# Paged decode attention: another place for the pages, another order of values and scores, a maximum per row

## The chip, the cores and the metric

One core of a Trainium2 chip runs the whole step as one program. The metric is the device time of one execution in microseconds; less is better.

## The reference

One step of a hybrid layer: a prompt of 1024 tokens and eight decode tokens go through a combined projection, latent attention beside a state-space mixer, an output projection, a mixture of experts and a last gate. The change touches only the attention of the eight decode tokens. Each of them (a "sequence") has 4096 cached tokens in 32 pages of 128, found by a page table; a cached token is a latent of 256 values and a rotary key of 32.

```python
past_ckv = cache_ckv[page_table].reshape(B, -1, KV_LORA)      # B = 8, 4096 x 256
past_kr = cache_krope[page_table].reshape(B, -1, QK_ROPE)     # 4096 x 32
q_lat = jnp.einsum('blhd,chd->blhc', q_nope, w_uk)            # 8 heads
s_past = (jnp.einsum('blhc,btc->bhlt', q_lat, past_ckv)
          + jnp.einsum('blhr,btr->bhlt', q_rope, past_kr)).astype(jnp.float32) * ATTN_SCALE
s_new = ...                                                   # the token itself
p = jax.nn.softmax(jnp.concatenate([s_past, s_new], axis=-1), axis=-1)
o_lat = (jnp.einsum('bhlt,btc->blhc', p[..., :T], past_ckv)
         + jnp.einsum('bhls,bsc->blhc', p[..., T:], ckv))
return jnp.einsum('blhc,chd->blhd', o_lat, w_uv)
```

The sum over cached tokens does not depend on their order, so a page may lie in memory in any way that scores and values share.

## The kernel before

The program is a row of stages (projection, prompt attention, decode attention, output projection, experts, last gate), each a block with an instruction stream per engine, written out by hand with semaphores; a barrier of all engines ends each. The decode stage (lines 1434 to 1681) begins at about 572 us and its last VectorE instruction ends at 783.55 us.

**Pages.** Eight pages make a group, four groups a sequence, 32 groups in all. A page is 128 tokens of 288 floats (147,456 bytes) and is one DMA (`load_pages`, line 1252): token p of the page goes to partition p, 1,152 bytes in each of 128 partitions. SP issues pages 0 to 3 of a group and POOL 4 to 7 (`SHARE`, line 1250); page numbers are read from the table into registers first. Groups 0 to 3 are loaded by SP alone during the prompt attention. The ring has 11 places (`RING3`). Group `at` from 11 on waits in `load_share` (line 1266) until the sequence that used its place is done with its values: `spv_mm` counts the sequences whose last matmul (line 1531) is finished. So the end of sequence b releases four groups: the last one of sequence b + 2 and the first three of sequence b + 3.

**Transposes.** VectorE turns each group (`turn_pages`, line 1617: one 32x32 block transpose of 128x2304) into `pgT`, which has room for one sequence; a group's half of `pgT` must have been scored before (`past_mm`).

**Scores.** `scores(b)` on TensorE (line 1483) works in 32x32 tiles in two halves of two groups each, 144 instructions a half, and then the new token (line 1496). They stand in four PSUM banks; partition 32 g + h holds head h for group g, so a head's scores are spread over four partitions.

**Softmax.** `largest(b)` on VectorE (line 1623) takes a maximum per partition (`smx`), with the new token's for heads. To make it one per head, TensorE transposes `smx` (`largest_row`, 1500), VectorE takes the maximum over the four parts (`row_bounds`, 1636), TensorE brings it back as a column (`bound_column`, 1504), and ACT copies it to `nb`. Only then does ACT take the exponentials (`exps`, 1580), with sums per partition in `rs`. TensorE turns the probabilities (`turn_probs`, 1508) and adds the sums of a head's four partitions, ACT copies the turned ones (`turned_probs`, 1592), VectorE takes the reciprocal and the new token's turned probabilities (`row_sums`, 1646).

**Values.** `weigh(b)` (line 1520) multiplies the turned probabilities with the pages as loaded, 32 matmuls of two instructions, and the new token (1531). ACT scales the result by the reciprocal (`latent_out`, 1598).

**Order.** On TensorE, for each b: scores of b, turning of b - 1, `largest_row` of b, first half of the values of b - 1, `bound_column` of b, second half of the values of b - 1. On VectorE: transposes 0 and 1 of sequence b + 1, maximum of b, sums of b - 1, `row_bounds` of b, transposes 2 and 3. On ACT: copy of the turned probabilities of b - 1, exponentials of b, scaled result of b - 1. Queues run in order, so an instruction that waits holds all behind it.

Of the kernel before, what the change touches and what calls it, by code (L numbers as in the profile page):

```python
# [78 lines left out]
def program(nc, t_in, t_out):  # L79
# [16 lines left out]
    with ExitStack() as ctx:  # L96
# [1155 lines left out]
        def load_pages(eng, name, at, first, some):  # L1252
# [3 lines left out]
            for m, page in enumerate(found):  # L1256
                eng.dma_start(group_pages(at)[:, first + m, :], cache[bass.ds(page, 1), :, :].rearrange("a p w -> (a p) w")).then_inc(page_sw[at % RING3] if name == "pool" else page_in[at % RING3], 16)  # L1257
# [188 lines left out]
        smx = sb_in(p3, "smx", [P, 1])  # L1446
# [6 lines left out]
        rs = sb_in(p3, "rs", [P, 2])  # L1453
# [19 lines left out]
        def _(pe):  # L1473
# [34 lines left out]
            def turn_probs(b):  # L1508
                pe.wait_ge(S("sexp_rdy"), 2 * b + 2)
                if b:  # L1510
                    pe.wait_ge(S("pT_rdy"), b)
                    pe.wait_ge(S("rden3_rdy"), b)
                for x in range(8):
                    last = pe.matmul(pb[:, 4, 32 * x:32 * x + 32], pexp[:, x, :, :].rearrange("p g t -> p (g t)"), heads, start=True, stop=True)
                last.then_inc(S("pT_tr"), 1)
                for m in range(2):
                    pe.matmul(pb[:, 5, H:H + 1], same[:, :, :].rearrange("p c r -> p (c r)"), rs[:, m:m + 1], start=m == 0, stop=m == 1, skip_group_check=True)
                pe.transpose(pb[0:32, 5, 0:H], pnew[:, :], ident[0:H, 0:H]).then_inc(S("sums_mm"), 1)

            def weigh(b, some):  # L1520
# [4 lines left out]
                for x in some:  # L1525
                    q = x % 4
                    last = pe.matmul(pb[32 * q:32 * q + H, 7, 0:KL], pT[b % 2][:, x % 8, x // 8, :], group_pages(4 * b + x // 8)[:, x % 8, 0:KL], start=x < 4,
                                     stop=x >= PAGES - 4 and q > 0, skip_group_check=True, tile_position=(0, 32 * q))
                if some[-1] == PAGES - 1:
                    pe.wait_ge(S("pTn_rdy"), b + 1)  # L1530
                    pe.matmul(pb[0:H, 7, 0:KL], pTn[:, :], ckvn[:, :], start=False, stop=True, skip_group_check=True,
                              tile_position=(0, 0)).then_inc(S("spv_mm"), 1)
# [1353 lines left out]
```

## Time and profile before

| | |
|---|---|
| median of three runs | 1594.5 us (1593.17 to 1598.28) |
| the profiled execution | 1593.95 us, its span 1592.3 us |
| decode stage in the trace | about 572 to 784 us |
| transposes of pages (line 1621) | 32, 81.8 us busy on VectorE, idle before them 83.4 us |
| matmuls of the scores (line 1492) | 2304, 79.1 us busy, idle before them 44.6 us |
| matmuls of the values (line 1527) | 512, 34.4 us busy |
| turning of the probabilities (line 1514) | 128, 15.8 us busy |
| exponentials (line 1588) | 8, 8.9 us busy |

Engines are PE (TensorE), PEld (its weight loads), DVE (VectorE), ACT, POOL and SP; a "q" behind a name is the engine's sequencer. In a timeline a line merges neighbouring instructions of one kind, with their number behind the x; "idle before" is what the engine waited and for whom. PEclk is the granted TensorE clock (1.0 is 2.4 GHz, 0.5 is 1.2 GHz).

### The profile page before, as it was taken

To read this page: it belongs to the slowest core of one execution; us is meant where nothing else is said; L and a number is where in the kernel's file an instruction comes from. 1 tells how busy PE (TensorE), PEld (TensorE's weight loads), DVE (VectorE), ACT (ScalarE), POOL (GpSimd) and SP (SyncE) were. 2 spreads that over 40 slices of the span, in tenths; PEclk is the share of its full clock that TensorE was granted. 3 is DMA by queue.
4 is the path that set the end of the run, shared out by engine and by line. 5 is a ranking of instruction groups with operands and counts; after the bars stand their busy time and mean duration, and the time that the engine had idled before them with its cause. 6 is when DMAs were issued, how large, how long until landed. Compare 5 with 4: busy or idle time off the path is not lost. (4 is left out here: it accounts for less than half of the span.)

```text
span 1592.3 us, 26749 instructions
## 1 busy us (share of the span) xinstructions
PE 1354.5 (85%) x9613; PEld 1084.7 (68%) x9613; DVE 979.7 (62%) x1338; ACT 638.1 (40%) x856; POOL 220.3 (14%) x322
## 2 busy tenths in 40 slices
PE   5989999786688877766789982899999999937997
PEld 4989999776344444333568872687888888825886
DVE  5456556663577765454244445788888888845653
ACT  5222434320366611101232100777777777743221
POOL 6000221051100032232000000000000000012210
PEclk9999999898799988878779995899999999977999
DMA  5121111375994055464262221479656999935410
GB/s 185 31 79 41 57 67 54 126 251 155 283 371 113 1 169 161 143 217 152 80 226 106 96 90 66 148 263 363 230 211 235 331 404 405 379 143 214 159 67 40
DMA packets 121049, 275.20 MB, mean 173 GB/s; under 512 B 23601, under 2 KB 44594, under 8 KB 120626
## 3 DMA queue, kind: packets, MB, share of 16 engines
q1 hardware_dynamic: 100578, 200.64, 37.1%
q0 software_dynamic: 17200, 61.63, 10.9%
q10 hardware_dynamic: 3168, 11.54, 1.8%
q8 instruction: 67, 1.10, 0.3%
q14 instruction: 36, 0.29, 0.1%
HBM read 214.34 MB, written 58.38 MB: 171 GB/s over the span
## 5 line engine op out<-in xcount | busy, mean ns | idle before, releaser
L399 PE MATMUL pb<-xH,wH 128*128 128x344 f32 x432 | 143.1, 331 | 25.1 <-DVE wL L858 11.0
L401 PE MATMUL pb<-xH,wL 128*128 128x344 f32 x432 | 140.8, 326 | 0.0
L400 PE MATMUL pb<-xL,wH 128*128 128x344 f32 x432 | 140.8, 326 | 0.0
L1621 DVE STREAM_TRANSPOSE pgT<-pages 128x2304 f32<-128x2304 f32 x32 | 81.8, 2570 | 83.4 <-DMA pages<-in_cache 74.5
L2463 DVE TENSOR_TENSOR downL<-raw_down,downH 128x2048 fp32r<-128x2048 f32 x44 | 98.9, 2288 | 45.2 <-ACT downH L2365 45.2
L1492 PE MATMUL pb<-pgT,q 32*8 32x256 f32 x2304 | 79.1, 432 | 44.6 <-DVE pgT L1621 41.9
L2365 ACT CAST gateH<-raw_gate 128x2048 fp32r<-128x2048 f32 x44 | 83.9, 1911 | 67.5 <-PE pb L2298 41.5
L2463 DVE TENSOR_TENSOR gateL<-raw_gate,gateH 128x2048 fp32r<-128x2048 f32 x44 | 100.5, 2287 | 15.8 <-ACT gateH L2365 15.8
L399 PEld LDWEIGHTS pb<-xH,wH 128*128 128x128 f32 x432 | 83.8, 194 | 27.3 <-issue 10.9
L2463 DVE TENSOR_TENSOR upL<-raw_up,upH 128x2048 fp32r<-128x2048 f32 x44 | 100.3, 2281 | 1.0 <-ACT upH L2365 1.0
L1492 PEld LDWEIGHTS pb<-pgT,q 32*8 32x8 f32 x2304 | 41.5, 94 | 81.8 <-DVE pgT L1621 44.9
L1321 PE MATMUL pb<-kh,qh 96*128 96x512 f32 (+3 forms) x192 | 75.8, 515 | 15.5 <-DMA vh<-v_d 14.5
L2365 ACT CAST upH<-raw_up 128x2048 fp32r<-128x2048 f32 x44 | 81.6, 1902 | 15.8 <-PE pb L2298 15.8
L400 PEld LDWEIGHTS pb<-xL,wH 128*128 128x128 f32 x432 | 83.7, 194 | 0.0
L401 PEld LDWEIGHTS pb<-xH,wL 128*128 128x128 f32 x432 | 83.6, 194 | 0.0
L2365 ACT CAST downH<-raw_down 128x2048 fp32r<-128x2048 f32 x44 | 81.6, 1909 | 0.0
L1257 POOL DMA_DIRECT2D pages<-in_cache x112 | 60.2, 538 | 117.2 <-issue 113.1
L2296 PE MATMUL pb<-gateH,hxH 128*128 128x512 f32 x176 | 73.5, 417 | 1.3 <-ACT sg L2378 0.7
L2296 PE MATMUL pb<-downH,axH 128*128 128x512 f32 x176 | 72.2, 410 | 1.6 <-DVE axL L2477 1.6
L2297 PE MATMUL pb<-gateL,hxH 128*128 128x512 f32 x176 | 71.3, 405 | 0.0
L2298 PE MATMUL pb<-gateH,hxL 128*128 128x512 f32 x176 | 71.0, 403 | 0.0
L1368 ACT ACTIVATE prob<-pb,nmx 128x128 f32<-128x128 f32 (+7 forms) x64 | 47.7, 745 | 57.8 <-DVE nmx L1402 56.6
(436 smaller groups left out, 3246.7 us busy)
## 6 DMA issues: line engine op xcount, KB each, us to landing
raw_gate<-in_w_gate SPq DMA_DIRECT2D x32, 1024.0 KB, 7.4
raw_up<-in_w_up SPq DMA_DIRECT2D x32, 1024.0 KB, 7.8
raw_down<-in_w_down SPq DMA_DIRECT2D x32, 1024.0 KB, 8.0
pages<-in_cache SPq DMA_DIRECT2D x144, 144.0 KB, 3.6
y_d<-yzero POOLq DMA_DIRECT2D x4, 4096.0 KB, 31.7
pages<-in_cache POOLq DMA_DIRECT2D x112, 144.0 KB, 3.7
y_d<-yo ACTq DMA_DIRECT2D x22, 512.0 KB, 4.1
wraw_p<-in_w_blk SPq DMA_DIRECT2D x18, 512.0 KB, 3.5
```

The source lines that it names most:

```text
L399: pe.matmul(out, wh, xh, start=first, stop=False)
L400: pe.matmul(out, wh, xl, start=False, stop=False)
L401: return pe.matmul(out, wl, xh, start=False, stop=last)
L1257: eng.dma_start(group_pages(at)[:, first + m, :], cache[bass.ds(page, 1), :, :].rearrange("a p w -> (a p) w")).then_inc(page_sw[at % RING3 ...
L1321: last = pe.matmul(pb[:, bank, 0:w], qh[b][n][:, i * P:(i + 1) * P], kh[b][n][:, 512 * m:512 * m + w], start=True, stop=True)
L1492: last = pe.matmul(pb[32 * g:32 * g + H, r, 0:256], q4[at, b, j, :], pgT[at, 8 * g:8 * g + 8, 32 * j:32 * j + 32], start=j == 0, stop=j == ...
L1621: dve.transpose(pgT[:, 8 * g:8 * g + 8, :], group_pages(4 * b + g)).then_inc(S("pgT_rdy"), 1)
L2296: pe.matmul(out, xh[:, k, :], high[w][:, k, a:b], start=first, stop=False)
L2297: pe.matmul(out, xh[:, k, :], low_[w][:, k, a:b], start=False, stop=False)
L2298: return pe.matmul(out, xl[:, k, :], high[w][:, k, a:b], start=False, stop=last)
L2365: act.copy(part(high[w], c), part(raw[w], c)).then_inc(S(w + "_high"), 1)
L2463: dve.tensor_tensor(part(low_[w], c), part(raw[w], c), part(high[w], c).bitcast(F32), ALU.subtract).then_inc(S(w + "_low"), 1)
```

## The change

A page goes into 32 partitions: page n of a group to the set 32 (n mod 4), with four tokens (4,608 contiguous bytes) in each partition. It is still one DMA per page, by the same queues.

Each partition keeps its own maximum: the exponentials take its negative (`nmx3`) and start without the head's maximum. That one is found in the same steps as before, but enters later as a factor per partition, exp of the partition's maximum less the head's (`part_w`, on ACT): the row sums are multiplied by it (`part_s`, on VectorE) before TensorE adds them, and the reciprocal is multiplied by it (`scale_rdy`).

The order on TensorE for each b becomes: second half of the values of b - 1, turning of b, `largest_row` of b, first half of the values of b, `bound_column` of b, scores of b + 1, sums of b. `spv_mm` counts halves. A half of the values is now four page columns of all four groups, so all places of a sequence are released by its second half. On VectorE one transpose instead of two stands ahead of the maximum, and the transpose of the new token's probabilities is copied by ACT instead of VectorE.

```diff
             for m, page in enumerate(found):
-                eng.dma_start(group_pages(at)[:, first + m, :], cache[bass.ds(page, 1), :, :].rearrange("a p w -> (a p) w")).then_inc(...)
+                n = first + m
+                dst = group_pages(at)[32 * (n % 4):32 * (n % 4) + 32, n // 4 * 4:n // 4 * 4 + 4, :]
+                eng.dma_start(dst, cache[bass.ds(page, 1), :, :].rearrange("a (p s) w -> (a p) s w", s=4)).then_inc(...)
...
             if at >= RING3:
-                eng.wait_ge(S("spv_mm"), (at - RING3) // 4 + 1)
+                eng.wait_ge(S("spv_mm"), 2 * ((at - RING3) // 4) + 2)
...
-                pe.transpose(pb[0:1, 6, 0:P], smx[:, :], ident).then_inc(S("smx_tr"), 1)
+                pe.transpose(pb[0:1, 6, 0:P], smx[:, b % 2:b % 2 + 1], ident).then_inc(S("smx_tr"), 1)
...
                 for x in range(8):
-                    last = pe.matmul(pb[:, 4, 32 * x:32 * x + 32], pexp[:, x, :, :]..., heads, start=True, stop=True)
-                last.then_inc(S("pT_tr"), 1)
+                    pe.matmul(pb[:, 4, 32 * x:32 * x + 32], pexp[:, x, :, :]..., heads, start=True, stop=True)
+                pe.transpose(pb[0:32, 4, 256:256 + H], pnew[:, :], ident[0:H, 0:H]).then_inc(S("pT_tr"), 1)
+
+            def sums(b):
+                pe.wait_ge(S("part_s_rdy"), b + 1)
                 for m in range(2):
-                    pe.matmul(pb[:, 5, H:H + 1], same..., rs[:, m:m + 1], start=m == 0, stop=m == 1, ...)
-                pe.transpose(pb[0:32, 5, 0:H], pnew[:, :], ident[0:H, 0:H]).then_inc(S("sums_mm"), 1)
+                    last = pe.matmul(pb[:, 5, H:H + 1], same..., part_s[:, m:m + 1], start=m == 0, stop=m == 1, ...)
+                last.then_inc(S("sums_mm"), 1)
...
                 for x in some:
-                    q = x % 4
-                    last = pe.matmul(pb[32 * q:32 * q + H, 7, 0:KL], pT[b % 2][:, x % 8, x // 8, :], group_pages(4 * b + x // 8)[:, x % 8, 0:KL], ...)
-                if some[-1] == PAGES - 1:
+                    for c in range(4):
+                        last = pe.matmul(pb[32 * c:32 * c + H, 7, 0:KL], pT[b % 2][:, x, c, :], group_pages(4 * b + c)[:, x, 0:KL], ...)
+                if some[-1] == 7:
                     pe.wait_ge(S("pTn_rdy"), b + 1)
...
-            largest_row(0)
-            bound_column(0)
-            for b in range(1, NB + 1):
-                if b < NB:
-                    scores(b)
-                turn_probs(b - 1)
-                if b < NB:
-                    largest_row(b)
-                weigh(b - 1, range(0, PAGES // 2))
-                if b < NB:
-                    bound_column(b)
-                weigh(b - 1, range(PAGES // 2, PAGES))
+            for b in range(NB):
+                if b:
+                    weigh(b - 1, range(4, 8))
+                turn_probs(b)
+                largest_row(b)
+                weigh(b, range(0, 4))
+                bound_column(b)
+                if b + 1 < NB:
+                    scores(b + 1)
+                sums(b)
+            weigh(NB - 1, range(4, 8))
...
             def exps(b):
+                act.wait_ge(S("nmx3_rdy"), b + 1)
...
+                act.activation(pexp..., past..., ACT.Exp, bias=nmx3[:, :], scale=SCALE, accum_out=rs[:, n, 0:1]).then_inc(S("sexp_rdy"), 1)
+                act.activation(pnew[:, :], snew_s[:, :], ACT.Exp, bias=nmx3[0:H, :], scale=SCALE, accum_out=rs[0:H, n, 1:2]).then_inc(S("sexp_rdy"), 1)
+
+            def part_weights(b):
                 act.wait_ge(S("nb_mm"), b + 1)
...
                 act.copy(nb[:, :], pb[:, 6, P:P + 1]).then_inc(S("nb_rdy"), 1)
...
+                act.activation(part_w[:, :], smx[:, b % 2:b % 2 + 1], ACT.Exp, bias=nb[:, :], scale=SCALE).then_inc(S("part_w_rdy"), 1)
 
             def turned_probs(b):
...
+                act.copy(pTn[0:32, :], pb[0:32, 4, 256:256 + H]).then_inc(S("pTn_rdy"), 1)
...
-            exps(0)
-            for b in range(1, NB + 1):
-                turned_probs(b - 1)
-                if b < NB:
-                    exps(b)
-                latent_out(b - 1)
+            for b in range(NB):
+                exps(b)
+                if b:
+                    latent_out(b - 1)
+                turned_probs(b)
+                part_weights(b)
+            latent_out(NB - 1)
...
+                dve.tensor_scalar(nmx3[:, :], smx[:, at], -SCALE, None, ALU.mult).then_inc(S("nmx3_rdy"), 1)
...
+            def part_sums(b):
+                dve.wait_ge(S("part_w_rdy"), b + 1)
...
+                dve.tensor_scalar(part_s[:, :], rs[:, b % 2, :], part_w[:, :], None, ALU.mult).then_inc(S("part_s_rdy"), 1)
+
+            def part_scales(b):
                 dve.wait_ge(S("sums_mm"), b + 1)
                 dve.reciprocal(rden3[:, b:b + 1], pb[:, 5, H:H + 1]).then_inc(S("rden3_rdy"), 1)
...
+                dve.tensor_tensor(rden3[:, b:b + 1], rden3[:, b:b + 1], part_w[:, :], ALU.mult).then_inc(S("scale_rdy"), 1)
...
                 if b + 1 < NB:
                     turn_pages(b + 1, 0)
-                    turn_pages(b + 1, 1)
                 largest(b)
                 if b:
-                    row_sums(b - 1)
+                    part_scales(b - 1)
+                if b + 1 < NB:
+                    turn_pages(b + 1, 1)
                 row_bounds(b)
                 if b + 1 < NB:
                     turn_pages(b + 1, 2)
+                part_sums(b)
+                if b + 1 < NB:
                     turn_pages(b + 1, 3)
-            row_sums(NB - 1)
+            part_scales(NB - 1)
```

## Rows read from the trace of the kernel before

**Rows 1.** First line of the page: the span.

```profile
span 1592.3 us, 26749 instructions
```

**Rows 2.** Table of waits, 555 to 790: waiter, line, released by: us, times, longest.

```profile
DVE pgT L1621 <- DMA pages<-in_cache: 74.5, 15, 11.6
```

**Rows 3.** Own waits of the DMA queue of SP, 400 to 800.

```profile
SPq L1254 <- PE pb L1531: 75.5, 6, 18.3
...
SPq L1426 <- PEq L1426: 59.6, 1, 59.6
```

**Rows 4.** Timeline of ACT, 575 to 800: start us, us, line, operation, idle before.

```profile
596.80 1.11 ACT L1588 ACTIVATE pexp<-pb,nb 128x1024 f32<-128x1024 f32 x1
...
616.61 0.47 ACT L1601 ACTIVATE wkv<-pb,rden 128x256 f32<-128x256 f32 x1 [0.56 <-PE pb L1531]
...
644.32 0.47 ACT L1601 ACTIVATE wkv<-pb,rden 128x256 f32<-128x256 f32 x1 [0.56 <-PE pb L1531]
...
689.81 0.37 ACT L1596 COPY pT<-pb 128x256 f32<-128x256 f32 x1 [18.05 <-PE pb L1514]
...
770.34 0.47 ACT L1601 ACTIVATE wkv<-pb,rden 128x256 f32<-128x256 f32 x1 [0.56 <-PE pb L1531]
...
776.76 0.47 ACT L1601 ACTIVATE wkv<-pb,rden 128x256 f32<-128x256 f32 x1 [4.14 <-PE pb L1531]
```

**Rows 5.** Timeline of all engines, 640 to 720, one round.

```profile
670.66 0.59 PE L1531 MATMUL pb<-ckvn,pTn 128*8 128x256 f32 x2
...
671.19 4.09 PE L1492 MATMUL pb<-pgT,q 32*8 32x256 f32 x144
...
679.25 2.58 DVE L1621 STREAM_TRANSPOSE pgT<-pages 128x2304 f32<-128x2304 f32 x1 [10.89 <-DMA pages<-in_cache]
...
681.88 5.35 PE L1492 MATMUL pb<-pgT,q 32*8 32x256 f32 x128 [6.60 <-DVE pgT L1621]
...
687.39 2.58 DVE L1621 STREAM_TRANSPOSE pgT<-pages 128x2304 f32<-128x2304 f32 x1 [2.16 <-DMA pages<-in_cache]
...
687.81 1.97 PE L1514 MATMUL pb<-cst,pexp 128*128 128x32 f32 x16
...
689.89 1.19 DVE L1628 TENSOR_REDUCE smx<-pb 128x1 f32<-128x1024 f32 x1
...
691.47 0.15 DVE L1634 TENSOR_TENSOR smx<-smx,colmx 8x1 f32<-8x1 f32 x1
...
691.87 3.35 PE L1527 MATMUL pb<-pages,pT 128*8 128x256 f32 x32
...
695.66 1.91 PE L1527 MATMUL pb<-pages,pT 128*8 128x256 f32 x32
...
697.39 0.59 PE L1531 MATMUL pb<-ckvn,pTn 128*8 128x256 f32 x2
```

**Rows 6.** Timelines of VectorE and TensorE, first and last sequence of the stage.

```profile
593.51 1.19 DVE L1628 TENSOR_REDUCE smx<-pb 128x1 f32<-128x1024 f32 x1
...
598.35 9.83 PE L1492 MATMUL pb<-pgT,q 32*8 32x256 f32 x271 [1.84 <-ACT pnew L1590]
...
763.35 1.22 DVE L1628 TENSOR_REDUCE smx<-pb 128x1 f32<-128x1024 f32 x1 [5.85 <-PE pb L1496]
...
783.36 0.19 DVE L1676 COPY attT<-pb 128x32 f32<-128x32 f32 x1 [2.00 <-PE pb L1562]
```

**Rows 7.** Timeline of SP in an early stage, 60 to 100.

```profile
80.42 0.72 SPq L330 DMA_DIRECT2D kt_d<-ev  x1
```

**Rows 8.** Stretches: busy us of each engine, PEclk, DMA share, GB/s.

```profile
577.00:601.00 24.00, 17.56 (x401) 9.80 (x407) 20.15 (x14) 2.82 (x7) 13.34 (x25) 0.71 0.98 314
82.00:87.00 5.00, 5.00 (x34) 5.00 (x32) 2.44 (x4) 0.00 (x0) 0.00 (x0) 1.00 0.97 199
87.00:88.00 1.00, 0.29 (x2) 0.00 (x1) 0.00 (x0) 0.00 (x0) 0.00 (x0) 1.00 1.01 373
...
647.00:652.40 5.40, 1.30 (x50) 0.56 (x32) 0.00 (x0) 0.00 (x0) 3.58 (x7) 0.89 0.95 284
```

More of the change, by code:

```diff
@@ L1445, in program @@
         snew_s = sb_in(p3, "snew_s", [H, 32])
-        smx = sb_in(p3, "smx", [P, 1])
+        smx = sb_in(p3, "smx", [P, 2])
+        nmx3 = sb_in(p3, "nmx3", [P, 1])
+        part_w = sb_in(p3, "part_w", [P, 1])
+        part_s = sb_in(p3, "part_s", [P, 2])
         mrow = sb_in(p3, "mrow", [1, 4, 32])
@@ L1511, in turn_probs @@
                     pe.wait_ge(S("pT_rdy"), b)
-                    pe.wait_ge(S("rden3_rdy"), b)
+                    pe.wait_ge(S("pTn_rdy"), b)
                 for x in range(8):
-                    last = pe.matmul(pb[:, 4, 32 * x:32 * x + 32], pexp[:, x, :, :].rearrange("p g t -> p (g t)"), heads, start=True, stop=True)
-                last.then_inc(S("pT_tr"), 1)
+                    pe.matmul(pb[:, 4, 32 * x:32 * x + 32], pexp[:, x, :, :].rearrange("p g t -> p (g t)"), heads, start=True, stop=True)
+                pe.transpose(pb[0:32, 4, 256:256 + H], pnew[:, :], ident[0:H, 0:H]).then_inc(S("pT_tr"), 1)
+            def sums(b):
+                pe.wait_ge(S("part_s_rdy"), b + 1)
                 for m in range(2):
-                    pe.matmul(pb[:, 5, H:H + 1], same[:, :, :].rearrange("p c r -> p (c r)"), rs[:, m:m + 1], start=m == 0, stop=m == 1, skip_group_check=True)
-                pe.transpose(pb[0:32, 5, 0:H], pnew[:, :], ident[0:H, 0:H]).then_inc(S("sums_mm"), 1)
+                    last = pe.matmul(pb[:, 5, H:H + 1], same[:, :, :].rearrange("p c r -> p (c r)"), part_s[:, m:m + 1], start=m == 0, stop=m == 1, skip_group_check=True)
+                last.then_inc(S("sums_mm"), 1)
             def weigh(b, some):
@@ L1525, in weigh @@
                 for x in some:
-                    q = x % 4
-                    last = pe.matmul(pb[32 * q:32 * q + H, 7, 0:KL], pT[b % 2][:, x % 8, x // 8, :], group_pages(4 * b + x // 8)[:, x % 8, 0:KL], start=x < 4,
-                                     stop=x >= PAGES - 4 and q > 0, skip_group_check=True, tile_position=(0, 32 * q))
-                if some[-1] == PAGES - 1:
+                    for c in range(4):
+                        last = pe.matmul(pb[32 * c:32 * c + H, 7, 0:KL], pT[b % 2][:, x, c, :], group_pages(4 * b + c)[:, x, 0:KL], start=x == 0,
+                                         stop=x == 7 and c > 0, skip_group_check=True, tile_position=(0, 32 * c))
+                if some[-1] == 7:
                     pe.wait_ge(S("pTn_rdy"), b + 1)
-                    pe.matmul(pb[0:H, 7, 0:KL], pTn[:, :], ckvn[:, :], start=False, stop=True, skip_group_check=True,
-                              tile_position=(0, 0)).then_inc(S("spv_mm"), 1)
+                    last = pe.matmul(pb[0:H, 7, 0:KL], pTn[:, :], ckvn[:, :], start=False, stop=True, skip_group_check=True,
+                                     tile_position=(0, 0))
+                last.then_inc(S("spv_mm"), 1)
             pe.wait_ge(S("q4_rdy"), 2)
```

46 lines of the change are left out of this document (28 added, 18 removed).

## The prediction

> **What bounds the kernel now.** One core, so I take the span first [rows 1]: 1592.3 us, with 1593.95 us for that execution as a whole, 0.55 us under the median of the runs (1594.5). Sums are made against 1593.95. The stages stand one behind the other with a barrier between them, so only the decode stage (about 572 to 784 us) has to be studied; what it loses or gains at its end moves everything behind it.
>
> The table of waits over that stage comes next [rows 2]: VectorE, which transposes each group of pages before TensorE can score it, waits 74.5 us for pages to land. The DMA queues' own waits give the other half [rows 3]: SP waits 75.5 us for the last matmul of the weighted values (line 1531), because a group of pages may be loaded only when the sequence that used its place is weighed. So the stage is a ring: values done, pages released, pages land, transpose, scores, values done. I call the end of line 1531 of sequence b T(b). It is also the moment from which ACT's line 1601 runs, and its eight starts read T(0) = 616.6 to T(6) = 770.3 [rows 4].
>
> The timeline of one round shows the pieces [rows 5]. T(2) is at 671.25 (end of the first row). The first released group, the last of the four of sequence 4, is landed and begins its transpose at 679.25: 8.0 us. Transpose to the start of the second half of the scores: 2.6 us (681.88). That half, new token included, ends at 687.8: 5.9 us. Turning the probabilities lasts to about 690.2. Then comes the part that this order costs: the transpose of 687.39 sits ahead of the maximum on VectorE, the maximum begins at 689.89 and is ready at 691.62, and only behind it does TensorE weigh, from 691.87 to 697.98. Sum 8.0 + 2.6 + 5.9 + 2.4 + 1.7 + 6.1 = 26.7 us, which is T(3) - T(2). The last three rounds take 24; the six together take 153.7 us.
>
> **The change, part by part.** *The order of work.* The second half of the values now follows directly on the scores of the next sequence, ahead of its probabilities; the first half is done before those scores. Behind the last-landing group the path is only: transpose 2.7 (handoff included), second half of the scores 5.9, the two sum matmuls 0.6, then 16 pages' values. These are 32 instructions of 1.91 us, plus line 1531, 0.59 us [rows 5]: 2.5. I keep 5.9 for the half although it contains a slow clock at its start; the first half, 144 instructions, took 4.09 us at the full clock [rows 5], so this term may be 1.2 us too long. Without the loading time, the round is 2.7 + 5.9 + 0.6 + 2.5 = 11.7 us, where it was 26.7 - 8.0 = 18.7.
>
> *Does the other chain fit beside it?* From the end of a sequence's scores: maximum 1.75 (689.89 to 691.62), its negative 0.15 (a 128x1 step), exponentials 1.55 (596.80 to the release of line 1492 at 598.35 [rows 4, 6]), turning 2.2 (1.97 and the small transpose), copy 0.4 [rows 4], first half of the values 1.9 to 3.35 by the clock, the bound column 0.4, the first half of the next scores 4.1: 12.4 to 13.9. The scores end 3.1 us ahead of T, so this chain reaches the second half of the scores at T + 9.3 to T + 10.8; the pages reach it at T + 11.7 (below). It fits, with 1 to 2 us to spare. That spare is the cover for everything I count at nothing: the copy of the new token's probabilities that goes from VectorE to ACT, the factor of each row on ACT (a 0.16 us copy and a small exponential), and the products on VectorE (0.15 each). New waits: VectorE's product of the sums waits for ACT's factor, and behind it is queued the transpose of the last group; the factor is ready about T + 7, ahead of the pages. TensorE's sums wait for that product, behind the next scores, long after it. If the cover were gone, these 1 to 2 us a round would be on the path: 6 to 12 us in all.
>
> *The pages in 32 partitions.* Each page is still one DMA of 147,456 B, but it goes to 32 partitions with 4,608 B in one piece in each, instead of 1,152 B in each of 128. The number of issues on SP and POOL stays, four each for a group. The trace has no such load, so the price is bounded. Slow end: the one large transfer on 32 partitions, the rotary-key store of 1 MB at 80.42 [rows 7], moved at 199 GB/s with the DMA engines busy 0.97, and the 128-partition weight loads queued right behind it went at 373 [rows 8]; both in pieces of 4 KB. Fast end: that 373, or at the least the pages' present 314 GB/s over seven groups [rows 8]. In flight are pages of two queues, each walking through four sets of partitions, POOL about one page behind. I take a mix by time of the slow row and the present rate, half the bytes at 199 and half at 314: 245 GB/s. A group (eight pages, 1.18 MB) then takes 4.8 us and the four of a round 19.3. Now the landing. In the round of T(1), 644.3 [rows 4], data moves from 647.0, 2.7 us behind it, and the first group is in at 652.4; these 5.4 us, at 284 GB/s [rows 8], move 1.54 MB (the second group's SP pages mix in). At 245 that is 6.3, so the landing is T + 9.0.
>
> The Trainium skill speaks against this part. "SBUF — State Buffer", section "Door 1: The DMA port swizzle", says that a transfer's rate goes by how many of 16 ports its partitions reach, and that 32 partitions reach eight; the section on two DMAs for both halves measured only 6% from a second transfer on the other half. The slow row agrees with the first; no run here shows the second. By it the rate would be 199 x 1.06 = 211 GB/s and the time about 1573 (an estimate).
>
> *The sum.* Round: 9.0 + 11.7 = 20.7 us, above the 19.3 that the transfers need. T(0): the scores of sequence 0 end 0.8 us before 593.51, as the maximum need not wait for the second transpose any more [rows 6]. From 592.7: 1.75 + 0.15 + 1.55 + 2.2 + 0.4 + 3.35 (slow clock behind the pause) + 0.4 + both halves of the next scores with the new token 10.3 (598.35 to 608.66) + 0.6 + 2.5 = 615.9, and some 0.6 for handoffs: 616.5, as now. The gain begins behind it. T(6) = 616.5 + 6 x 20.7 = 740.7; the scores of sequence 7 end 3.1 earlier, 737.6, where before they ended at 763.2 [rows 6]. Tail: from there to the last copy (783.55) 20.4 us before; after it, 1.75 + 0.15 + 1.55 + 2.2 + 0.4 + 1.9 + 0.4 + 1.9 (the factor, product and sums, for which the rest of the values now waits) + 2.5 + 0.6 for the scaled copy + 6.35 (from 777.2, the end of that copy [rows 4], to 783.55) = 19.7. Gain 25.6 + 0.7 = 26.3, so 1593.95 - 26.3 = 1567.7, or 1568 us.
>
> Loads of the first four groups lie in the stage before; SP then waits 59.6 us for TensorE [rows 3], so even at 199 GB/s (23.7 us instead of 15) they cost nothing; without that cover they would cost 9 us.
>
> **The rivals.** *The pages run at the slow row's rate.* Both queues walk the same sets of partitions in step, and all transfers together get 199 to 211 GB/s. Then transfers set the pace: 28 groups, 33.0 MB, from 577 at 201 take 164 us; the last lands at 742, transpose and scores 8.6, tail 19.7: 770.6 instead of 783.55, so 1581 (1573 at 211). For it speaks the one row on 32 partitions; against it, that it was one transfer on one set of partitions. The skill's rule above is this rival.
>
> *Slower than before.* The same mechanism with loads that are below the store: a page is only 144 KB, so that no long run hides the start of each, or its row is still cut into 1,152 B pieces. The point from which it decides: the last group must land by 755.3 for the old end, so 33.0 MB in 177.3 us, 186 GB/s. At 175 GB/s it lands at 766.7, the stage ends at 795 and the time is 1605. Against it: the store reached 199.
>
> *The wide rows pay and the partitions don't matter.* At 314 GB/s the landing is T + 7.6 and the round 19.3: T(6) = 732.3, time 1559. Faster still, the landing drops out and the chain beside it sets the round: 12.4 + 5.9 = 18.3, T(6) = 726.3, time 1553. For it: the 373 row, and that pages of different sets are in flight together.
>
> *The change doesn't give its order.* A new wait closes the spare: the bound column on TensorE waits for VectorE behind the transpose of a late group, and the scores start 6 us later than I have them. Round 3.1 + 12 + 4.1 + 5.9 = 25.1, T(6) = 767, time 1594. Against it: in the rows those groups are landed a round earlier.
>
> **How the numbers follow.** Forecast (215 to 300 GB/s, 1561 to 1573) 0.42; slow rate (1573 to 1586) 0.24; wide rows pay (1553 to 1561) 0.20; slower 0.08; order lost 0.06. The range from 1555 to 1586 takes in the first three but for their ends, 0.8. A measurement of this kernel tells about 0.3% (5 us) from no change: faster by more than that are the first three and a little of the last, 0.87; within, the rest of the last, 0.05; slower 0.08.
>
> **What would show it.** Right: the starts of ACT's scaled copy about 20.7 us apart; the first transposed group 9 us behind them; DMA rate of 240 or so with the share near 1 in the loading stretches; second-half values directly behind the scores; as many issues on SP and POOL as before. Wrong: DMA share at 1 without a gap over the whole stage and about 200 GB/s (the slow rate); TensorE waiting for the bound column or the exponentials for more than 3 us a round (order lost); rounds of 18 to 19 us with gaps in the DMA row (wide rows pay).

## The result, and the profile after

The changed kernel takes 1583.97 us (median of four runs, 1580.35 to 1585.39) beside 1594.05 for the kernel before on the same chip: a ratio of 0.9922 with a 95% interval from 0.9902 to 0.9942. It is faster by 10 us, at the late end of the range from 1555 to 1586, where 1568 was forecast: the forecast gain was 26 us. The profiled execution took 1584.53 us; its span is 1582.9, against 1592.3 [rows 1].

In the kernel before, it took 201.2 us from the first score instruction of the stage to the start of its last copy (582.19 to 783.36 [rows 6]); in the changed kernel it takes 194.9 (578.23 to 773.10), 6.3 less. Another 4.0 us of this execution's gain lie ahead of that: the first score instruction starts earlier (first line before, second after), and 3.3 of them are there at the first matmul of the stage already (572.2 before, 568.9 after). Behind the stage 0.9 us are lost. Over the kernels of this study the start scatters from 578 to 586 us (589 in shift, which adds work ahead of it), so the 4.0 us are not shown to come from the change, and lengths below are counted from the first score instruction.

```profile
582.19 8.95 PE L1492 MATMUL pb<-pgT,q 32*8 32x256 f32 x252 [0.68 <-ACT q L1606]
```

```profile
578.23 9.74 PE L1497 MATMUL pb<-pgT,q 32*8 32x256 f32 x252 [0.68 <-ACT q L1626]
```

The waits over 555 to 790 us in the changed kernel (waiter, line, released by: us, times, longest):

```profile
DVE pgT L1642 <- DMA pages<-in_cache: 39.1, 17, 4.8
...
PEld pb L1497 <- issue: 25.8, 49, 4.5
...
PE pb L1497 <- issue: 13.1, 5, 4.0
```

The wait for pages has nearly halved against [rows 2], as the new order should do. New is the last line: TensorE's matmuls stand in the middle of the scores with every semaphore satisfied, waiting for nothing but its own next instruction ("issue"), up to 4.0 us at a time; before, the longest such wait was 0.2 us on the matmuls. The timeline of TensorE shows them in place (start, length, line, count; the idle time before stands in brackets):

```profile
590.95 1.49 PE L1497 MATMUL pb<-pgT,q 32*8 32x256 f32 x24 [2.97 <-issue]
...
635.10 0.60 PE L1497 MATMUL pb<-pgT,q 32*8 32x256 f32 x8 [4.02 <-issue]
...
695.64 5.60 PE L1497 MATMUL pb<-pgT,q 32*8 32x256 f32 x128 [1.96 <-issue]
...
704.85 2.77 PE L1497 MATMUL pb<-pgT,q 32*8 32x256 f32 x48 [3.61 <-issue]
...
734.73 0.39 PE L1535 MATMUL pb<-pages,pT 128*8 128x256 f32 x3 [2.47 <-issue]
```

With 0.52 us at 626.43 they sum to 15.5 us. T(b), the end of the values of sequence b, is read as in [rows 4], from ACT's scaled copy and TensorE's line 1539: 616.2, 642.2, 663.9, 685.0, 714.0, 735.3, 754.4. The rounds are 26.0, 21.6, 21.2, 29.0, 21.3 and 19.1 us, 23.0 on the average, against 25.6 before and 20.7 forecast. The long ones, 26.0 and 29.0, are those with waits of 4.5 and 5.6 us. A round without a wait, T(2) to T(3), in the timeline of all engines:

```profile
663.26 0.59 PE L1539 MATMUL pb<-ckvn,pTn 128*8 128x256 f32 x2
...
673.71 2.58 DVE L1642 STREAM_TRANSPOSE pgT<-pages 128x2304 f32<-128x2304 f32 x1 [2.79 <-DMA pages<-in_cache]
...
676.35 5.23 PE L1497 MATMUL pb<-pgT,q 32*8 32x256 f32 x128 [2.63 <-DVE pgT L1642]
...
682.69 1.91 PE L1535 MATMUL pb<-pages,pT 128*8 128x256 f32 x32
...
684.42 0.59 PE L1539 MATMUL pb<-ckvn,pTn 128*8 128x256 f32 x2
```

Released at 663.85, the last-landing group begins its transpose at 673.71 (9.9 us later; 9.0 forecast), its scores start 2.6 later, the values are done at 685.0: 21.2 us, half a microsecond over the forecast round. Against [rows 5] the values now follow directly on the scores.

The stretches (busy us of PE, PEld, DVE, ACT, POOL with instructions, then PEclk, DMA share, GB/s), to be held against [rows 8]:

```profile
577.00:601.00 24.00, 16.42 (x323) 10.18 (x322) 11.92 (x10) 2.09 (x5) 10.48 (x22) 0.64 1.03 268
...
640.00:660.00 20.00, 15.84 (x334) 8.85 (x334) 9.42 (x7) 1.99 (x9) 7.87 (x16) 0.86 0.78 172
660.00:680.00 20.00, 16.26 (x365) 9.54 (x356) 11.62 (x15) 2.73 (x9) 7.87 (x16) 0.91 1.00 221
680.00:700.00 20.00, 16.94 (x380) 9.46 (x367) 12.15 (x14) 2.73 (x9) 7.48 (x16) 0.92 1.02 226
700.00:720.00 20.00, 16.13 (x276) 8.90 (x268) 10.22 (x13) 2.85 (x9) 2.79 (x6) 0.74 0.61 144
```

From 620 us on, where the DMA engines are full they move 221 to 226 GB/s; the opening stretch, with seven groups issued at once, moved 268. The stretches of 172 and 144 GB/s hold the late T(1) and T(4): a late end of values releases pages late, and the engines run dry. The last row of these has a granted clock of 0.74.

In the view of DMA issues over 577 to 770 (issues, KB each, median us from issue to landing) the time to landing has doubled: a page of the kernel before lands 3.5 to 3.7 us behind its issue, one of the changed kernel 7.3 to 7.4. First two lines before, last two after:

```profile
pages<-in_cache POOLq DMA_DIRECT2D x109, 144.0 KB, 3.7
pages<-in_cache SPq DMA_DIRECT2D x108, 144.0 KB, 3.5
```

```profile
pages<-in_cache POOLq DMA_DIRECT2D x106, 144.0 KB, 7.3
pages<-in_cache SPq DMA_DIRECT2D x104, 144.0 KB, 7.4
```

### The profile page after: what moved, and what is told of

It is laid out like the page before. It is cut to its first block and busy times, and to the rows that moved or that the text cites. A ratio compares the mean times of both kernels' runs of the same rounds, so it can differ in the third digit from the quotient of the medians.

```text
span 1582.9 us, 26802 instructions
## 1 busy us (share of the span) xinstructions
PE 1363.7 (86%) x9613; PEld 1090.6 (69%) x9613; DVE 982.5 (62%) x1354; ACT 640.8 (40%) x872; POOL 215.4 (14%) x322
## 5 line engine op out<-in xcount | busy, mean ns | idle before, releaser
L1259 POOL DMA_DIRECT2D pages<-in_cache x112 | 55.2, 493 | 114.6 <-issue 107.5
```

Source lines behind the costliest of these rows:

```text
L1259: eng.dma_start(dst, cache[bass.ds(page, 1), :, :].rearrange("a (p s) w -> (a p) s w", s=4)).then_inc(page_sw[at % RING3] if name == "pool ...
```

## The experiments

The change has three parts: the place of the pages, the order, and the maximum per row. Theory 1 was that the place costs what the order gains; theory 2, that TensorE's waits for its own instructions beside full DMA engines hold the new order back, wherever the pages lie.

**The order and the row maximum without the new place (order_only).** The changed kernel with the loads of before:

```diff
-                dst = group_pages(at)[32 * (n % 4):32 * (n % 4) + 32, n // 4 * 4:n // 4 * 4 + 4, :]
-                eng.dma_start(dst, cache[...].rearrange("a (p s) w -> (a p) s w", s=4))...
+                eng.dma_start(group_pages(at)[:, first + m, :], cache[...].rearrange("a p w -> (a p) w"))...
```

> The changed kernel with the pages as before, 1,152 bytes in each of 128 partitions; the order of work and the maximum per row stay changed. Theory 1, the placement of the pages is what holds the change back (222 GB/s in the loading stretches instead of 314): data moves at 300 GB/s or more, the first released group is transposed about 8.2 us behind the end of the values, rounds are about 20 us and the time is about 1565. Theory 2, TensorE's waits for its own instructions beside full DMA engines hold it back, whatever the placement: waits of 2 to 4 us within the scores stay, rounds are 22 us or more and the time stays within 5 us of the changed kernel (1579 to 1589).

Measured: 1554.95 us, ratio 0.9752 (0.9721 to 0.9783), 10 us under what theory 1 expected. The scaled copies of ACT and two stretches:

```profile
658.37 0.45 ACT L1619 ACTIVATE wkv<-pb,rden 128x256 f32<-128x256 f32 x1
676.36 0.45 ACT L1619 ACTIVATE wkv<-pb,rden 128x256 f32<-128x256 f32 x1
695.51 0.45 ACT L1619 ACTIVATE wkv<-pb,rden 128x256 f32<-128x256 f32 x1
```

```profile
660.00:680.00 20.00, 17.35 (x419) 10.97 (x422) 13.96 (x17) 3.17 (x11) 10.38 (x20) 0.99 0.84 264
680.00:700.00 20.00, 17.87 (x420) 10.36 (x412) 13.64 (x15) 2.75 (x9) 8.63 (x16) 0.93 0.79 248
```

Rounds of 18.0 and 19.2 us here, 18.6 over the whole row of copies, with DMA engines at 0.8: not loads but the chain of maximum, exponentials, turning and values sets the round now (over 577 to 770 TensorE waits 10.1 us for exponentials and 2.1 us for transposed pages). The prediction's fastest case had that chain at 18.3 us and a time of 1553. TensorE's waits for instructions are all under 1 us. The order, with the row maximum, gives what that fastest case had, and the new place takes 29 us of it away (1584.0 less 1555.0).

**The new place alone (pages_only).** The kernel before with the three changed lines of `load_pages`.

> The kernel before with the pages in 32 partitions and nothing else changed. Theory 1: the pages move at about 220 GB/s, the landing of the first released group comes 1.5 to 3 us later in each of six rounds, and the time is 1602 to 1610. Theory 2: TensorE is idle while pages land in this order, so that its instructions arrive in time; the placement alone costs at most 5 us (1594 to 1599).

Measured: 1631.78 us, ratio 1.0237 (1.0204 to 1.027), 37 us slower than before and more than either theory expected. The wait for pages, over 555 to 830 as this stage ends later:

```profile
DVE pgT L1623 <- DMA pages<-in_cache: 104.8, 16, 13.5
```

It was 74.5 us [rows 2]. The place costs in either order.

**POOL's pages on the other sets (far_sets).** In the changed kernel both queues walk the sets of 32 partitions in the same sequence. Here POOL's pages go to sets 2, 3, 0, 1.

```diff
-                dst = group_pages(at)[32 * (n % 4):32 * (n % 4) + 32, ...]
+                c = (n + 2 * (n // 4)) % 4
+                dst = group_pages(at)[32 * c:32 * c + 32, ...]
```

> The changed kernel, with POOL's four pages of a group on the sets of partitions in the order 2, 3, 0, 1, where SP's go to 0, 1, 2, 3. If the two queues walking the same sets in step is what makes the pages slow, the loading stretches rise from 222 to 280 GB/s or more and the time falls to about 1572. If a transfer into 32 partitions is slow by itself, the rate stays at 215 to 230 GB/s and the time within 4 us of the changed kernel. Theory 2 expects the waits for instructions to stay in either case as long as the DMA engines are full.

Measured: 1581.59 us, ratio 0.9922 (0.99 to 0.9945), the same as the changed kernel. One stretch moves 238 GB/s (share 0.96), but others 217 (0.96) and 224 (1.02, the opening one, where the changed kernel had 268), and TensorE's waits grow to 21.5 us, the longest 5.7. Walking in step is not the price. The Trainium skill, "SBUF — State Buffer", section "Can I just issue two DMAs to hit both halves?", has 6% for a second transfer on the other half; stretches that scatter from 217 to 238 against 221 to 226 neither show such a gain nor rule it out.

**Pieces or partitions (short_pieces, sets64).** The same 32 partitions, but four pieces of 1,152 bytes in each; and 64 partitions with one piece of 2,304 bytes in each.

```diff
-... cache[...].rearrange("a (p s) w -> (a p) s w", s=4)
+... cache[...].rearrange("a (s p) w -> (a p) s w", s=4)
```

> The changed kernel, but a page goes into its 32 partitions as four runs of 32 tokens: each partition gets four separate pieces of 1,152 bytes (token 32 s + p to partition p) instead of one piece of 4,608. If the set of partitions is what slows the loads: about 222 GB/s in the full stretches as in the changed kernel, its full DMA share, TensorE's waits for its own instructions of 2 to 4 us, and about 1584 us or a little more. If it is the length of the piece: the rate goes back to 265 to 314 GB/s, the waits vanish, and 1555 to 1565 us. If both count: slower than 1584, the pieces cost a start each, up to 1630.

```diff
-                dst = group_pages(at)[32 * (n % 4):32 * (n % 4) + 32, n // 4 * 4:n // 4 * 4 + 4, :]
-                ... "a (p s) w -> (a p) s w", s=4
+                dst = group_pages(at)[64 * (n % 2):64 * (n % 2) + 64, n // 2 * 2:n // 2 * 2 + 2, :]
+                ... "a (p s) w -> (a p) s w", s=2
```

> The changed kernel, but a page goes into 64 partitions with two tokens (2,304 bytes in one piece) in each. If the rate goes by the number of partitions that one page reaches: between the 222 GB/s of 32 partitions and the 265 and more of 128, about 250 GB/s, and some 1565 to 1572 us. If 64 partitions are no better than 32 (an estimate after the Trainium skill, SBUF - State Buffer, section Door 1: The DMA port swizzle, says the same ports are reached): 222 GB/s or 4% more, and 1578 to 1584 us. If half the width is as good as the whole: 1555 us.

Measured: 1581.54 us (0.9877 to 0.994 of before) and 1570.74 us (0.9816 to 0.9864). Stretches of both, first short_pieces, then sets64:

```profile
620.00:640.00 20.00, 16.43 (x383) 9.48 (x386) 10.79 (x13) 0.93 (x5) 8.82 (x16) 0.88 0.99 234
...
660.00:680.00 20.00, 16.59 (x368) 9.46 (x356) 11.90 (x15) 2.73 (x9) 8.78 (x16) 0.91 0.99 236
```

```profile
640.00:660.00 20.00, 17.16 (x399) 10.37 (x399) 12.91 (x15) 2.80 (x10) 8.36 (x16) 0.91 0.94 231
660.00:680.00 20.00, 17.33 (x373) 9.98 (x376) 9.96 (x8) 0.87 (x4) 8.36 (x16) 0.83 0.99 237
```

Quartering the piece changes little: 234 to 236 GB/s in these stretches, waits of 16.6 us in sum, the same time. With the same pieces of 1,152 bytes, pages in 128 partitions land in 3.6 us (order_only) and pages in 32 in 6.7 to 7.0: it is the set of partitions that costs, not the length of the piece. With 64 partitions 237 GB/s move at a share of 0.99, up to 7% more than with 32 in the changed kernel and no more than in short_pieces, and TensorE's waits are 12.2 us. The Trainium skill, "SBUF — State Buffer", section "Door 1: The DMA port swizzle", says that 64 partitions reach no more ports than 32, with 4% more measured; the rates here, 0 to 7% more, do not speak against it. The time, 13 us under the changed kernel, is that which was expected of a rate by the number of partitions, and it does not follow from this rate; 3.3 us less of waits stand for a part of it. From 620 to 720 us the DMA share in sets64 stays at 0.85 or more, where the changed kernel's falls to 0.78 and 0.61; why is open.

**What the row maximum is worth (head_max, max_only).** head_max is order_only with exponentials that wait for the head's maximum as before; max_only is the maximum per row in the order of before; both with the pages in 128 partitions. (In head_max VectorE's `row_bounds` moves up as well, and the factor of a row is one, its products left in. In max_only ACT and VectorE are put back in the sequence of before.)

```diff
-                turn_probs(b)
                 largest_row(b)
-                weigh(b, range(0, 4))
                 bound_column(b)
+                turn_probs(b)
+                weigh(b, range(0, 4))
...
-                act.wait_ge(S("nmx3_rdy"), b + 1)
+                act.wait_ge(S("nb_mm"), b + 1)
...
-                act.activation(pexp..., bias=nmx3[:, :], ...)
+                act.activation(pexp..., bias=nb[:, :], ...)
```

> The new order with the pages in 128 partitions, but the exponentials wait for the maximum of the head as before the change (found and brought back as a column ahead of the turning, and the factor of a row set to one). If the chain of maximum, exponentials and turning fits beside the landing of the pages, as the prediction had it with 1 to 2 us to spare, two transposes and a copy more (about 2 us a round) take that spare up and little more: 1555 to 1560 us. If the chain already sets the round in the new order (rounds of 18.6 with the DMA engines busy 0.8): 2 us a round more and 2 in the tail, 1569 to 1573 us.

```diff
+            largest_row(0)
+            bound_column(0)
+            for b in range(1, NB + 1):
+                if b < NB:
+                    scores(b)
+                turn_probs(b - 1)
+                sums(b - 1)
+                if b < NB:
+                    largest_row(b)
+                weigh(b - 1, range(0, 4))
+                if b < NB:
+                    bound_column(b)
+                weigh(b - 1, range(4, 8))
```

> The maximum per row with its factor, in the order of before and with the pages of before in 128 partitions. If the parts add up: the new order alone gave 1577 and order with row maximum 1555, so the row maximum is worth 22 us here too, about 1572 us. If the maximum per row pays only in the new order (in the order of before the values of a sequence come a sequence later than its exponentials, so that the return of the head's maximum is beside other work): 1588 to 1595 us. If its added steps (factor, product, product of the reciprocal) land on the path: 1596 to 1605 us.

Measured: 1576.94 us (0.9855 to 0.9921), later than either expectation, and 1594.25 us (0.998 to 1.0015), as expected of a maximum that pays in the new order only. So of the 39 us of order_only the order alone gives 18 and the maximum per row alone nothing, as was expected where it is beside other work. In the new order it is worth 22, more than the 2 us a round of its own steps. The turning and the first half of the values on TensorE in one round, first order_only, then head_max:

```profile
658.51 1.97 PE L1517 MATMUL pb<-cst,pexp 128*128 128x32 f32 x16 [0.84 <-ACT pnew L1595]
...
661.05 1.91 PE L1533 MATMUL pb<-pages,pT 128*8 128x256 f32 x32 [0.26 <-ACT pT L1611]
```

```profile
659.36 3.62 PE L1517 MATMUL pb<-cst,pexp 128*128 128x32 f32 x16 [1.78 <-ACT pnew L1599]
...
663.56 3.60 PE L1533 MATMUL pb<-pages,pT 128*8 128x256 f32 x32 [0.46 <-ACT pT L1611]
```

The idle time of TensorE ahead of the turning doubles from 0.84 to 1.78 us, and both pieces behind it take 3.3 us more in this round: the granted clock over them is 0.50 (1.2 GHz) in head_max and 1.00 (2.4 GHz) in order_only. This round shows the most of it, since six of the eight first halves of order_only are slow too (3.15 to 3.6 us). Over the rounds of T(0) to T(6) the turning starts 2.0 us later behind T(b) (2.83 to 3.01 instead of 0.79 to 1.01), and turning and first half together take 6.3 us on the average instead of 4.9. Rounds are 18.6 us in the one kernel and 21.6 in the other: the later start and the slower clock are enough for that, and a part of them is made up elsewhere in the round.

**Full DMA engines without slow pages (order_more).** order_only, with each page of SP copied a second time to device memory that nobody reads.

```diff
+            if name == "sp" and at >= 4:
+                for m, page in enumerate(found):
+                    eng.dma_start(twice[4 * at + m, :, :], cache[...])...
```

> The new order with the pages in 128 partitions, and each page of SP is also copied to a place in device memory that nobody reads, so that half as many bytes again go through the same DMA engines. Adds traffic, leaves nothing out. If full DMA engines are what makes TensorE wait for its own instructions: waits of 2 to 4 us in the middle of the scores appear here too, 10 us and more in the stage, and the granted clock falls to 0.5 behind them. If it is the slow packets of pages in 32 partitions: no such wait over 1 us, as without the extra copies, though the stage becomes longer (42 MB and more at 265 to 314 GB/s, 160 to 190 us), 1555 to 1580 us.

Measured in one run: 1590.19 us; the longer rounds are those of the added bytes. The only wait for instructions over 0.15 us in the scores is the first line; the second is a stretch at 311 GB/s:

```profile
588.63 0.86 PE L1500 MATMUL pb<-pgT,q 32*8 32x256 f32 x24 [0.77 <-issue]
```

```profile
640.00:660.00 20.00, 14.31 (x343) 7.31 (x343) 8.25 (x7) 0.63 (x4) 6.47 (x12) 0.74 0.94 311
```

Engines busy to 0.82 to 0.94 with quick pages don't hold TensorE's instructions up. In these stretches the share does not reach the 1.0 of the changed kernel, but ahead of the wait of 0.77 us it does: 1.00 at 343 GB/s from 582.0 to 588.6. Every kernel has a wait at that same number of the instruction count (the next table), in the midst of the first loads. It is 0.7 us in one_flight, where the share there is 0.58. In all others the share is 0.95 to 1.05 in the 3 to 7 us ahead of it, and the wait is 0.2 to 0.8 us in the five kernels with pages in 128 partitions and 1.1 to 5.7 us in the seven with pages in fewer (2.97 in the changed kernel). So full engines alone are not the cause.

**What the waits are (shift).** Counting TensorE's records of the trace from the start of the execution (weight loads, matmuls and its own semaphore and register instructions; the place is good to one or two), every wait of the matmuls for "issue" over 0.15 us in the stage, in every kernel, stands at 193 to 195 modulo 256. Seven of these kernels:

```
kernel         place of each wait (number of the instruction), modulo 256   sum, us
before         6849                                        193               0.2
after          6851 8129 8385 10433 10689 11713            195, else 193    15.5
order_only     6849 8385 10689 11457 11713                 193               2.8
pages_only     6593 6849 8385 9153 9921                    193              11.9
far_sets       6593 6849 8385 9665 9921 10689 10945 11457  193              21.5
one_flight     6849 9665                                   193               2.0
order_more     6849                                        193               0.8
```

The sums go with the time that a page takes from issue to landing: up to 4.6 us where it lands in 3.0 to 4.4 us (all kernels with 128 partitions, and one_flight; the 4.6 are head_max, its longest wait 1.4), 9.5 where it lands in 5.0 (flight2), and 11.9 to 21.5 where it takes 5.6 to 7.7.

To tell the supply of instructions from something about these matmuls, shift does 32 matmuls of the step ahead of the stage twice: 128 instructions more (some 3 us).

```diff
+            for j in range(4):
+                for h in range(H):
+                    last = pe.matmul(pb[0:32, 6, ...], ukt[:, h, 32 * j:32 * j + 32], qd[:, h, :], start=True, stop=True)
             last.then_inc(S("qlat_mm"), 1)
```

> The changed kernel with 32 matmuls of the step before the stage done twice (128 more instructions on TensorE ahead of the scores, about 3 us ahead of the stage). In all kernels so far each wait of TensorE for its own instructions stands at position 193 modulo 256 when TensorE's instructions are counted from the start. If it is the supply of instructions, in blocks of 256: every such wait still stands at 193 modulo 256 with the added ones counted, so at places in the scores 128 instructions earlier than before; their sum stays near 15 us (10 to 20), and the time is 3 us more, 1584 to 1592. If a wait belongs to the instruction where it stands (its operands or its place in the scores): the same matmuls as in the changed kernel wait, which are now at 65 modulo 256.

Measured in one run: 1595.71 us, over the expected 1584 to 1592; of the 11 us more than in the changed kernel's trace 7.5 are there at the first matmul of the stage already (576.4 instead of 568.9), 3.5 are the added matmuls, and from the first score instruction on the stage is only 1.1 us longer. The waits stand at 6849, 8385, 8641, 9153, 9409, 10177, 10946 and 12225, again at 193 modulo 256 (one at 194), with 21.4 us in sum, a little over the 10 to 20 expected. So other matmuls wait than in the changed kernel, the values among them:

```profile
645.79 1.25 PE L1538 MATMUL pb<-pages,pT 128*8 128x256 f32 x12 [4.18 <-issue]
...
672.45 1.90 PE L1538 MATMUL pb<-pages,pT 128*8 128x256 f32 x16 [4.67 <-issue]
```

Both lie ahead of a release of pages, and the round of the second took 28.2 us (647.89 to 676.11). It is the supply of instructions, in blocks of 256. The DMA view of the changed kernel over 577 to 770 shows the blocks (packets, MB, share), 0.43 MB in 26 packets being 16.5 KB each:

```profile
q8 instruction: 26, 0.43, 1.0%
```

The Trainium skill, "Runtime: NRT & Kernel Launch", section "Instruction fetch mechanics", says that a sequencer gets its instructions in blocks of 16 KiB (256 of them) by a DMA queue of its own, and calls the crossing mostly hidden. The blocks agree; hidden they are in the kernel before (0.2 us), and not beside pages in 32 partitions.

**Fewer pages in flight (one_flight, flight2).** The changed kernel, with a group issued only when the group before it has landed, and when the one two before it has.

```diff
+            if at >= 5:
+                pages_in(eng, at - 1)
```

> The changed kernel, where SP and POOL issue a group only after the group before it has landed, so that at most one group is in flight. Theory 2, if TensorE's waits for instructions come from transfers queued on the same DMA engines: the waits of 2 to 4 us with no releaser within the scores fall under 1 us, though pages come later (each group about 7 us, four in 28 us, time 1600 to 1630). If these waits have another cause they stay, five or six of them, 10 us or more in all.

```diff
+            if at >= 6:
+                pages_in(eng, at - 2)
```

> The changed kernel, but a group is issued only when the group two before it has landed, so that at most two groups are in flight where there were up to four. If a long queue of pages ahead of them delays TensorE's instructions: the waits fall from 15.5 us to under 5, the DMA engines stay near full (200 GB/s or more in the stretches of loading), and the time drops to 1570 to 1578 us. If the slow packet itself does it, whatever stands in the queue: waits of 10 us and more remain and the time is the same or later, 1584 to 1600. If two groups do not fill the DMA engines (at most one gave 122 to 148 GB/s): rate 180 GB/s or less, 1610 us and more.

Measured: one_flight 1663.93 us in one run, beyond the 1600 to 1630 expected, with waits of 2.0 us in sum, but only 122 to 148 GB/s at a share of 0.49 to 0.59: the engines starve. flight2 takes 1572.91 us, ratio 0.9857 (0.9812 to 0.9902), 11 us under the changed kernel with the same bytes to the same places:

```profile
620.00:640.00 20.00, 16.81 (x400) 10.09 (x399) 12.71 (x15) 2.73 (x9) 7.85 (x16) 1.00 0.96 226
640.00:660.00 20.00, 17.05 (x378) 9.26 (x381) 10.36 (x9) 0.87 (x4) 7.86 (x16) 0.83 1.00 227
...
680.00:700.00 20.00, 16.69 (x395) 9.75 (x388) 11.70 (x14) 2.73 (x9) 6.95 (x15) 0.91 1.01 225
700.00:720.00 20.00, 16.95 (x337) 9.09 (x344) 12.02 (x15) 2.73 (x9) 7.45 (x16) 0.83 1.02 223
```

```profile
634.51 0.43 PE L1499 MATMUL pb<-pgT,q 32*8 32x256 f32 x8 [1.02 <-issue]
```

The engines stay full at the same 223 to 227 GB/s but for one stretch (213 at 0.92), the waits fall from 15.5 to 9.5 us, none but the first (2.42) over 2 us; the wait of 4.02 us at instruction 8385 is one of 1.02 here. The scaled copies run from 619.44 to 745.15, 21.0 us a round: four groups of 1.18 MB at 225 GB/s take just that. I had expected under 5 us of waits and 1570 to 1578 us; the time fell as that theory says, the waits only in part. A released group does not come sooner for it: the first one is transposed 8.6 to 11.1 us behind T(b), in the changed kernel 8.6 to 10.2. So the depth of the queue counts, and something is left that goes with the slow pages.

## Why the prediction was off

*The ring, and the order.* Right. The wait for pages shrank and the values follow on the scores. With the pages' old rate the prediction had 1559, and 1553 once the chain beside sets the round; order_only measured 1555.0 with rounds of 18.6 us.

*The spare beside.* The prediction gave the other chain 12.4 to 13.9 us and counted the row maximum's steps at nothing for 1 to 2 us of spare, with 6 to 12 us in all if that cover went. In the changed kernel the cover held: TensorE still waited 1.65 to 3.90 us for the last transpose in four of the six rounds. In order_only, where this chain sets the round, 2 us a round of added steps (head_max) cost 22 us: behind the longer pause on TensorE more of the work runs at the lower clock, which the prediction had in the range of one term (1.9 to 3.35) only.

*The rate.* Taken as 245 GB/s; the full engines of the changed kernel move 221 to 226. This term is small: the landing came 9.9 instead of 9.0 us behind T(b), the undisturbed round was 21.2 instead of 20.7, and flight2, which all but keeps to this, took 1572.9 instead of 1568. The mix by time of a slow and a fast row was 9% too high (and 244 rather than 245 when worked out). The slow rival's 199 to 211 GB/s were 6 to 11% too low. Its times (1573 to 1586) hold the measured 1584, but not for its reason: it wanted full engines throughout, and the changed kernel has stretches of 0.78 and 0.61 in the middle of the loading. The last landings of this rival and of the slower one were put 1 us late: 577 + 164 is 741, and from 577 to 755.3 are 178.3 us (185 GB/s). In flight2 the transfers do set the pace.

*The step that failed* is the sum itself: it has no term for what slow pages do to the supply of TensorE's instructions, and so puts it at nothing without a reason. Counted from the first score instruction, T(0) came 38.0 us after it, not 34.3 (616.5 less 582.19); the six rounds took 138.2 us, not 124.2; the last scores (751.6) ended 2.8 us ahead of T(6), not 3.1; and from there to the end of the last copy (773.3) it took 21.7, not 19.7. That is 3.7 + 14.0 + 0.3 + 2.0 = 20.0 us of forecast gain not found; 4.0 us came back by the earlier start and 0.9 were lost behind the stage, which leaves the 9.4 us of the span instead of 26.3. Ahead of T(0) stands one wait of 2.97 us; within the six rounds the waits are 12.6 (0.52 + 4.02 + 1.96 + 3.61 + 2.47), and without them, if each microsecond of wait cost one, the rounds would be 125.6 us, or 20.9 each. The tail's 2.0 is mostly the clock: the first half of the last values took 3.37 us where 1.9 was put, at a granted clock of 0.54.

```profile
757.81 3.37 PE L1535 MATMUL pb<-pages,pT 128*8 128x256 f32 x32 [0.26 <-ACT pT L1613]
```

flight2, which differs in the groups in flight alone, shows 11 us of the miss to go with the queue of pages and with 6 us less of waits. That each microsecond of wait is one of time is not shown: far_sets and shift have 6 us more of waits than the changed kernel, the one at the same time, the other in a stage only 1.1 us longer. What a wait costs seems to go by whether the late end of values lets the DMA engines run dry, as in the two stretches of 0.78 and 0.61, where flight2 stays at 0.92 or more from 620 to 720 us; this is argued from these stretches and not tested by itself.

*Its list of signs.* "DMA share near 1 and about 240 GB/s in the loading stretches" came out at 1.0 and 224; of the signs for being wrong, "DMA share at 1 without a gap" did not come, since gaps (0.78, 0.61) follow the waits. No sign was listed for a wait on "issue", the one that appeared.

*The lesson in price.* The new place costs 37 us alone and 29 in the new order, and buys nothing in this kernel that the old place does not have. The version with order and row maximum alone, 1555 us, beats both.

*Still open:* why a block of instructions is late beside pages in 32 partitions. It is later with a deeper queue (flight2 against the changed kernel) and where pages take longer to land, and far less with full engines and quick pages (order_more, and the start of the stage in all kernels with pages in 128 partitions); through which engine or buffer was not tried.

## What to carry to other kernels

In this kernel a layout that doubled a load's time to landing was paid for twice: in the rate, and in the instructions of the busiest engine, which came late beside such loads; so look for waits on "issue" at equal distances in the instruction count, and limit the loads in flight to what just keeps the DMA engines full. Judge the parts of a change singly and in pairs: here one part was worth 18 us, one nothing by itself but 22 on top of the first, and one minus 29. Where a chain has only a microsecond or two of spare, price its loss with the slow clock behind the pause, not with the steps alone.

## What the runs showed of the hardware that was not expected

Waits of TensorE for its own instructions, 0.2 us in the stage before and up to 5.7 us beside slow loads, always at 193 or so modulo 256 of its instructions. They cost again behind them: the 48 score instructions behind the 3.61 us wait took 2.77 us at a granted clock of 0.50, and the same 48 behind a 0.93 us wait in order_only took 1.50 at 1.00:

```profile
689.79 1.50 PE L1495 MATMUL pb<-pgT,q 32*8 32x256 f32 x48 [0.93 <-issue]
```

The granted clock over 700 to 720 us is 0.74 in the changed kernel and 0.83 in flight2, whose pauses are shorter. And a page in 32 partitions took 7.3 us from issue to landing with up to four groups in flight, where the same bytes over 128 partitions took 3.6.
